# First units of four root-mean-square layers on rows before normalization, and rotary tables made in the short convolution

## The chip, the core and the metric

One core of a Trainium2 chip runs the whole program, once. The metric is the device time of one execution in microseconds (us). The engines are TensorE (PE in the rows; PEld is its weight load), VectorE (DVE), ScalarE (ACT), GpSimd (POOL) and SyncE (SP), which issues the transfers. Each has its own queue and works it off in order; they wait for each other on semaphores.

## The reference, cut to what matters

Two blocks follow each other on 256 tokens of width 1024. The first has four layers, each `x = x + mixer(rms_norm(x, g))`:

- a0 and a1, a conformer convolution: three projections to 2048 channels, `val * sigmoid(gate)`, a causal depthwise convolution of 31 taps, a layer norm over the channels, SiLU, a product with `silu(z)`, and an output projection;
- b, attention with 16 heads and forget gates: q and k are normalized per head, the cumulated log forget gates are added to the scores, and a gate z multiplies the heads' output;
- c, a short convolution: `y = b_gate * conv3(c_gate * u)`, times `silu(z)`, then the output projection.

`rms_norm(x, g)` is `x * rsqrt(mean(x*x) + 1e-6) * g`, with one factor for each token (row). So a projection of a normalized row is the projection of `x * g`, multiplied afterwards by the row's factor.

The second block has two layers of a token mixer (m0, m1), which uses rotary embeddings, and a gated convolution feed-forward (f0, f1). Their shifts, scales and gates come from `silu(c) @ w_ada`, 96 dot-product pieces that do not depend on x. All is computed in float32.

## The kernel before

**Weights.** All weights are cut into pieces of up to 128x1024 values, in an order that the planners (plan_a at line 202, plan_b at 225, plan_c at 254, plan_f at 341) write out. SyncE loads them into six raw buffers (load, 423). A piece of the kind "split" is used as two parts in a reduced format: ScalarE casts it to the high part (line 113, tile wh), VectorE subtracts that from the raw piece to get the low part (line 120, tile wl, in feed_dve, 476). A "plain" piece is used raw. An "ada" piece is a modulation product, one VectorE operation (ada, 490, tile raw<-raw,cb). The feeds look three pieces ahead by default, with five buffers of each part. TensorE multiplies high by high, high by low and low by high; so a unit of 128 outputs has 24 matmuls of 256 columns (unit, 516), or eight float32 matmuls for a plain unit (plain_unit, 566), each recorded twice. token_major (575) turns the roles round: twelve matmuls of 512 columns for each piece.

**Activations.** The layer's normalized, transposed input lies in XS as a high part xh(k) and a low part xl(k) for k from 0 to 7 (128 channels each). The residual stream X lies by tokens: half(tb, h) is token block tb, 512 channels of half h.

**A layer's entry.** The last output piece is added up in quarters (tb, h) in the order (0,0), (0,1), (1,0), (1,1) (out_last, 605). VectorE adds each to X (dve_residual, 760). ScalarE squares each quarter with its sum (act_squares), VectorE and ScalarE make the root R (act_root 632, dve_root 636), both scale X by it (act_rms 742, dve_rms 768), TensorE transposes the scaled rows (pe_entry, 685), and ScalarE and VectorE write xh and xl from PSUM, multiplied by g. For the a layers VectorE first writes a plain copy xn, from which the parts are made. Only then does the first unit start. While this goes on, TensorE runs filler matmuls on constants: 15 for b, 16 for c, 14 for a1. Before a0 it runs 24 on a constant tile.

**What follows.** In a, eight pairs of gate and value units feed VectorE and ScalarE, whose taps and GpSimd's make the convolution (dve_a 1056). In b (pe_b 1469), the forget-gate piece b.f comes first, then three value chunks v0 to v2, four k, four q. In c (pe_c 1780) each step i takes two channel groups through c, u, b and z units, with two output pieces, in banks that VectorE must have folded. In its last step, i = 14, one SiLU and one product serve both groups, and then come their high and low parts. The rotary tables are made in a0, after the low parts, by VectorE (dve_rope, 1242) and two Sin on ScalarE (act_rope, 1279), in tmp tiles. The order of the work of each engine is written out by hand in these functions.

A term that comes back below: b.v1.0 is the first piece of the second value chunk; "c.b0.1" the second unit of the b gate at i = 0.

Of the kernel before, what the change touches and what calls it, by code (L numbers as in the profile page):

```python
# [8 lines left out]
F32 = mybir.dt.float32  # L9
# [7 lines left out]
T = 256  # L17
D = 1024
# [183 lines left out]
def plan_a(j):  # L202
# [22 lines left out]
def plan_b():  # L225
    out = [("b.f", [("b_w_in", 0, 128 * k, 128, 4 * E, 16) for k in range(8) for _ in range(2)], "split")]
# [9 lines left out]
    for n in range(3):  # L236
        chunk("v", n, 2 * E, (1, 2, 3) if n else (3,))
    for which, base in (("k", E), ("q", 0)):
        for n in range(4):
            chunk(which, n, base, (1, 3))  # L240
# [13 lines left out]
def plan_c(u, u1):  # L254
# [6 lines left out]
    for i in range(0, 16, 2):  # L261
        if i == 0:
            for n in range(2):
                for kind, base in (("c", 2 * E), ("u", 0)):
                    out.append((f"c.{kind}0.{n}", tiles("c_w_in", 0, base + n * 128), "split"))
                    if kind == "u":
                        ada()
        for kind, base in (("c", 2 * E), ("u", 0), ("b", E), ("z", 3 * E)):
# [10 lines left out]
            ada()  # L279
# [97 lines left out]
class Net:  # L377
# [148 lines left out]
    def first_units(self, pe, X, normed, units):  # L526

        made = [(self.weights(pe, name), name, out) for name, out in units]
        for k in range(8):
            pe.wait_ge(*self.s["xlow"][X, k])  # L530
            for (i, wh, wl), name, out in made:
                h, l = wh[:, k * 128:(k + 1) * 128], wl[:, k * 128:(k + 1) * 128]
# [5 lines left out]
            for n in range(8):  # L538
                if X[0] in "mf" and self.turned_after(X, n) == k:
                    self.pe_turned_late(pe, X, normed, n)  # L540

# [62 lines left out]

    def out_last(self, pe, L, ks, Ys):

        for tb in range(2):
            for h in range(2):
                for k, Y in zip(ks, Ys):
                    ins = self.out_part(pe, L, k, ks[-1] + 1, Y, tb, h)  # L610
                    names = [(L, "sum", tb, h)] if k == ks[-1] else []
                    if tb and h:
                        names += [self.at[f"{L}.o{k}"], (L, "out", k)]
                    if names:
                        ins.then_inc(self.s["gemm"].up(*names), 1)
# [42 lines left out]
    def turned_at(self, L):  # L658

        if L == "a0":  # L660
            return [(4, 0), (5, 0), (6, 0), (0, 0), (1, 0), (2, 0), (3, 0), (5, 1)]
        if L == "b":
            return [(n, 0) for n in (6, 4, 5, 7, 0, 1, 2, 3)]
        if L == "a1":
            return [(n, 0) for n in (4, 5, 6, 7, 0, 1, 2, 3)]
        if L == "c":
            return [(n, 0) for n in (4, 6, 7, 0, 1, 2, 3)] + [(6, 1)]
        return [(6 if L[0] == "m" else 4, 0), (0, 0), (1, 0), (2, 0), (3, 0), (0, 1), (1, 1), (2, 1)]

    def turned_after(self, L, k):  # L670

        if L[0] in "mf":
            return k - 4 if k > 4 else None
        return 1 if k == 7 and L in ("a0", "c") else None
# [10 lines left out]
    def pe_entry(self, pe, L, normed):  # L685
# [3 lines left out]
        self.warm(pe, {"a0": 0, "a1": 14, "b": 15, "c": 16, "m0": 0, "m1": 18}.get(L, 11))  # L689
# [6 lines left out]
        if L[0] in "ac":  # L696
            for k in late:
                self.pe_turned_late(pe, L, normed, k)
# [20 lines left out]
    def read_turned(self, L, k):  # L719

        s = self.s
        if L[0] == "a":
            return s["norm"][L, "xn", k]
        if L[0] in "bc":
            return s["xlow"][L, k]
        return s["evac"][L, "h", k] if k % 2 else s["norm"][L, "h", k]

    def xnt(self, tb, h):
        return self.tmp[2 * tb + h]

    def act_squares(self, act, L, ready):
        s = self.s
        act.table(ACT.Sqrt)
        for tb in range(2):
            for h in range(1 if tb and L == "a0" else 2):
# [6 lines left out]
    def act_rms(self, act, L, ready, gname, plain):  # L742
        s, R = self.s, self.sums("R")
        self.act_squares(act, L, ready)
        act.wait_ge(*s["norm"][L, "root"])
        for n in range(2):
            act.activation(self.xnt(1, 0)[:, 256 * n:256 * n + 256], self.half(1, 0)[:, 256 * n:256 * n + 256], ACT.Identity,
                           scale=R[:, 1:2]).then_inc(s["shift"].up((L, n)), 1)
        act.activation(self.xnt(1, 1), self.half(1, 1), ACT.Identity, scale=R[:, 1:2]).then_inc(
            s["shift"].up((L, 2), (L, 3)), 1)  # L750
        for k in range(8):
            if plain:
                act.wait_ge(*s["norm"][L, "xn", k])
                act.copy(self.xh(k), self.xn()[:, k, :]).then_inc(s["high"].up((L, k)), 1)
            else:
                act.wait_ge(*s["turn"][L, "in", k])
                act.activation(self.xh(k), self.turned_tile(L, k), ACT.Identity, scale=self.c(gname, k)).then_inc(
                    s["high"].up((L, k)), 1)

    def dve_residual(self, dve, P):  # L760
        s = self.s
        for tb in range(2):
            for h in range(2):
                o = self.half(tb, h)
                dve.wait_ge(*s["gemm"][P, "sum", tb, h])
                dve.tt(o, o, self.ps[2 * tb + h], ALU.add).then_inc(s["resid"].up((P, tb, h)), 1)

    def dve_rms(self, dve, L, gname, plain):
        s = self.s
        q, a, v, R = self.sums("q").rearrange("p (b h) -> p b h", b=2), self.sums("a"), self.sums("v"), self.sums("R")  # L770
        dve.wait_ge(*s["square"][L, 1, 0])
        dve.ts(a, q[:, :, 0], 1.0 / D, 1e-6, ALU.mult, ALU.add).then_inc(s["norm"].up((L, "a")), 1)
        dve.wait_ge(*s["norm"][L, "a"])
        dve.wait_ge(*(s["norm"][L, "q"] if L == "a0" else s["square"][L, 1, 1]))
        dve.stt(v, q[:, :, 1], 1.0 / D, a, ALU.mult, ALU.add).then_inc(s["norm"].up((L, "v")), 1)
        self.dve_root(dve, R, v, self.sums("d"), L)
        dve.wait_ge(*s["norm"][L, "root"])
        for h in range(2):
            dve.ts(self.xnt(0, h), self.half(0, h), R[:, 0:1], None, ALU.mult, None).then_inc(
                s["norm"].up((L, "x", 0, h)), 1)  # L780
        for k in range(8):
            dve.wait_ge(*s["turn"][L, "in", k])
            if plain:
                dve.ts(self.xn()[:, k, :], self.turned_tile(L, k), self.c(gname, k), None, ALU.mult, None).then_inc(
                    s["norm"].up((L, "xn", k)), 1)
            else:
                dve.wait_ge(*s["high"][L, k])
                dve.stt(self.xl(k), self.turned_tile(L, k), self.c(gname, k), self.xh(k).bitcast(F32), ALU.mult,
                        ALU.subtract).then_inc(s["xlow"].up((L, k)), 1)
        for k in range(8) if plain else ():  # L790
            dve.wait_ge(*s["high"][L, k])
            dve.tt(self.xl(k), self.xn()[:, k, :], self.xh(k).bitcast(F32), ALU.subtract).then_inc(
                s["xlow"].up((L, k)), 1)
# [50 lines left out]
    def pe_a(self, pe, j):  # L844
        s, A = self.s, f"a{j}"
        XN = self.xn()
        if j == 0:
            w = self.tmp[5][:, 0:128]
            pe.wait_ge(*s["fill"][0])
            for _ in range(24):  # L850
# [2144 lines left out]
```

## Time and profile before

| | us |
|---|---|
| median of 3 runs | 1757.71 (1756.76 to 1759.4) |
| the profiled execution, own time | 1757.96 |
| its span, first to last instruction | 1756.1 |
| TensorE busy | 1723.6 |
| VectorE busy | 1477.3 |
| ScalarE busy | 1094.9 |
| GpSimd busy | 289.7 |

Busy time counts filler matmuls too. A row's "idle before" is time in which the engine had nothing to run, with the operation whose end released it. In rows of a timeline the first two numbers are the start, from the start of the span, and the time to the end of the last of the instructions that the row joins. Since a matmul's modelled end overlaps the next one's start, the distance of two starts is what one costs.

### The profile page before, as it was taken

The numbers are of one execution on the slowest core, as the hardware profiler recorded it, in microseconds if no ns is written. First come the engines' busy times: TensorE is split into PE (matmuls) and PEld (weight loads), VectorE is DVE, ScalarE is ACT, GpSimd is POOL, SyncE is SP. The second block draws the span as 40 slices with busy tenths as digits, with TensorE's granted clock in tenths as the row PEclk, the third lists the DMA queues.
The fourth block names the chain that finished last, engine by engine and source line by source line (L and its number), as shares of the span: only waits on it lengthen the run. The fifth ranks groups of instructions, "written<-read, shape, count | busy, mean of one in ns | idle before, by whom it ended". The sixth has DMA issues, their size and how long they took to land.

```text
span 1756.1 us, 28780 instructions
## 1 busy us (share of the span) xinstructions
PE 1723.6 (98%) x10458; PEld 1510.2 (86%) x10458; DVE 1477.3 (84%) x2861; ACT 1094.9 (62%) x2149; POOL 289.7 (16%) x396
## 2 busy tenths in 40 slices
PE   9999999999999999999999999999999999999997
PEld 8888888888888888788898988988888998988886
DVE  7998878877789999788987698789987688789887
ACT  6888665555455555578875555566566656566664
POOL 3996000000000000078920000002000200002000
PEclk9999999999999999999999999999999999999999
DMA  6455568855558888544465654546764544546662
GB/s 239 153 157 172 170 220 305 266 179 183 201 196 315 289 304 310 170 154 136 153 194 157 224 185 133 170 148 189 253 223 146 168 156 127 174 143 188 222 187 78
DMA packets 92734, 339.49 MB, mean 193 GB/s; under 512 B 10288, under 2 KB 10672, under 8 KB 91952
## 3 DMA queue, kind: packets, MB, share of 16 engines
q1 hardware_dynamic: 92592, 337.64, 59.0%
q8 instruction: 84, 1.38, 0.3%
q14 instruction: 58, 0.48, 0.1%
HBM read 336.55 MB, written 1.05 MB: 192 GB/s over the span
## 4 chain that ended last, share of the span: by engine, by line
PE 74%; DVE 12%; ACT 8%; issue 4%; POOL 2%; DMA 0%; ACTq 0%; DVEq 0%; POOLq 0%
PE ps L104 72%; DVE wl L120 4%; ACT tmp L110 4%; ACT wh L113 2%; PE ps L107 2%; POOL B L120 2%; DVE tmp L130 1%; DVE raw L130 1%; DVE tmp L120 1%; DVE B L120 1%; DVE sm L142 1%; ACT os L113 1%; ACT B L110 1%; DVE os L120 1%; DVE X L130 0%
## 5 line engine op out<-in xcount | busy, mean ns | idle before, releaser
L104 PE MATMUL ps<-XS,wh 128*128 128x256 f32 (+2 forms) x3184 | 779.2, 327 | 8.6 <-DVE wl L120 4.7
L120 DVE TENSOR_TENSOR wl<-raw,wh 128x1024 fp32r<-128x1024 f32 x471 | 576.2, 1237 | 99.7 <-ACT wh L113 97.5
L104 PE MATMUL ps<-XS,wl 128*128 128x256 f32 x2152 | 581.7, 281 | 0.0
L104 PEld LDWEIGHTS ps<-XS,wh 128*128 128x128 f32 (+1 forms) x3184 | 525.3, 190 | 65.1 <-issue 19.0
L113 ACT CAST wh<-raw 128x1024 fp32r<-128x1024 f32 x471 | 479.5, 1044 | 102.3 <-PE ps L104 93.0
L104 PEld LDWEIGHTS ps<-XS,wl 128*128 128x128 f32 x2152 | 408.4, 190 | 11.5
L120 POOL TENSOR_TENSOR B<-B,tmp 128x236 f32<-128x236 f32 (+11 forms) x368 | 247.4, 716 | 642.0 <-ACT tmp L110 627.1
L104 PE MATMUL ps<-wh,os 128*128 128x512 f32 x864 | 280.8, 393 | 5.4 <-DVE os L120 4.1
L130 DVE SCALAR_TENSOR_TENSOR ps<-B,C,ps 128x253 f32<-128x253 f32 (+17 forms) x560 | 216.3, 465 | 2.8 <-ACT ps L110 2.8
L104 PE MATMUL ps<-B,raw 128*128 128x256 f32 x992 | 218.6, 380 | 0.0
L104 PEld LDWEIGHTS ps<-B,raw 128*128 128x128 f32 x992 | 186.7, 190 | 27.5 <-issue 2.9
L104 PEld LDWEIGHTS ps<-wh,os 128*128 128x128 f32 x864 | 162.9, 189 | 39.1 <-DVE os L120 5.0
L110 ACT ACTIVATE B<-ps 128x256 f32<-128x256 f32 (+2 forms) x216 | 95.4, 452 | 157.5 <-PE ps L104 157.2
L104 PE MATMUL ps<-wh,XS 128*128 128x512 f32 x576 | 179.4, 391 | 0.0
L110 ACT ACTIVATE tmp<-B,C 128x236 f32<-128x236 f32 (+11 forms) x368 | 153.8, 478 | 34.8 <-POOL B L120 34.0
L104 PE MATMUL ps<-wl,os 128*128 128x512 f32 x432 | 168.8, 391 | 0.0
L120 POOL TENSOR_TENSOR X<-X,B 128x512 f32<-128x512 f32 x24 | 42.1, 1754 | 700.5 <-PE ps L104 700.5
L104 PEld LDWEIGHTS ps<-wh,XS 128*128 128x128 f32 x576 | 107.2, 188 | 21.6
L130 DVE SCALAR_TENSOR_TENSOR raw<-raw,cb 128x1024 f32<-128x1024 f32 x96 | 116.3, 1217 | 0.0
L104 PE MATMUL ps<-wl,XS 128*128 128x512 f32 x288 | 112.3, 390 | 0.0
L104 PEld LDWEIGHTS ps<-wl,os 128*128 128x128 f32 x432 | 81.6, 189 | 16.7
L130 DVE SCALAR_TENSOR_TENSOR tmp<-ps,C,tmp 128x254 f32<-128x254 f32 (+1 forms) x176 | 76.1, 476 | 10.9 <-ACT tmp L110 8.8
(168 smaller groups left out, 1659.0 us busy)
## 6 DMA issues: line engine op xcount, KB each, us to landing
raw<-in_w SPq DMA_DIRECT2D x628, 512.0 KB, 4.5
B<-in_ln SPq DMA_DIRECT2D x4, 1024.0 KB, 6.7
C<-in_cst SPq DMA_DIRECT2D x1, 1103.5 KB, 9.1
X<-in_x SPq DMA_DIRECT2D x2, 512.0 KB, 4.5
out_x<-X SPq DMA_DIRECT2D x4, 256.0 KB, 2.5
cb<-in_cb SPq DMA_DIRECT2D x1, 512.0 KB, 13.7
pos<-in_pos SPq DMA_DIRECT2D x1, 160.0 KB, 5.3
raw<-in_w SPq DMA_DIRECT2D x1, 128.0 KB, 2.0
```

What stands on the lines that cost most here:

```text
L104: return NOTHING if self.e is None else self.e.matmul(*a, **k)
L107: return NOTHING if self.e is None else self.e.transpose(*a)
L110: return NOTHING if self.e is None else self.e.activation(*a, **k)
L113: return NOTHING if self.e is None else self.e.copy(*a)
L120: return NOTHING if self.e is None else self.e.tensor_tensor(o, a, b, op)
L130: return self.e.scalar_tensor_tensor(out=o, in0=a, scalar=s, in1=b, op0=op0, op1=op1, **k)
L142: return NOTHING if self.e is None else self.e.tensor_reduce(o, a, AX, ALU.max)
```

## The change

- Order of the quarters for the layers ahead of b, c and a1: (0,0), (1,0), (0,1), (1,1), with four raw transposes (k = 0 to 3) of the un-normalized X ahead of the last quarter. The other four come inside the first units. The filler of b, c and a1 goes; a0 has 18 instead of 24.
- The first units multiply `x * g` without the row factor: g0 in the a layers, v0 in b, the first units of c and u in c. Their results are multiplied by the factor afterwards: in b per token where v0 leaves PSUM, in a by an extra product ahead of the sigmoid, in c by the factor's square after `c * u`.
- The factor is spread over the partitions by two matmuls (pe_row_root) and copied by ScalarE. VectorE multiplies a kept copy of `x * g` by it (dve_normed), and in b and c xh and xl are then overwritten with the parts of the normalized rows while the first units read them (signals "bn", "cn").
- b.f moves from ahead of v0 to behind v1, and the forget row's work with it. In a1 v0's two pieces become plain.
- In c the ada pieces of i = 0 and two each of i = 4 and i = 8 are taken out of the order; they come later.
- The rotary tables move from a0 to c (VectorE at i = 4 and 8, ScalarE at i = 6), in tile G.
- At i = 14 in c the two groups are taken separately through SiLU, product, high and low parts.

```diff
 def plan_a(j):
-        first = "split" if j else "plain"
-        two("g", p, E, *[first if p == 1 else "plain"] * 2)
-        two("v", p, 0, "split" if p else first, "plain" if p else first)
+        two("g", p, E, *["split" if j and p == 1 else "plain"] * 2)
+        two("v", p, 0, "split" if p else "plain", "plain")
...
 def plan_c(u, u1):
-                    if kind == "u":
-                        ada()
...
-            ada()
+            if i and (i not in (4, 8) or kind in "uz"):
+                ada()
...
+    def quarters(self, L):
+        return ((0, 0), (1, 0), (0, 1), (1, 1)) if L in ("a0", "b", "c") else ((0, 0), (0, 1), (1, 0), (1, 1))
+
     def out_last(self, pe, L, ks, Ys):
+        for tb, h in self.quarters(L):
+            if tb and h and L in ("a0", "b", "c"):
+                for k in range(4):
+                    self.pe_raw_turned(pe, {"a0": "b", "b": "c", "c": "a1"}[L], k)
...
+    def pe_raw_turned(self, pe, L, k):
+        s, h, a = self.s, k // 4, (k % 4) * 128
+        if L != "a0" and k >= 4:
+            pe.wait_ge(*s["resid"][self.prior(L), 1, 1])
+        for tb in range(2):
+            pe.wait_ge(*(s[f"x{tb}"][0] if L == "a0" else s["resid"][self.prior(L), tb, h]))
+            ins = pe.transpose(self.turned_tile(L, k)[:, tb * 128:tb * 128 + 128], self.half(tb, h)[:, a:a + 128],
+                               self.c("ident", 0, 128))
+        ins.then_inc(s["turn"].up((L, "in", k)), 1)
+
+    def pe_row_root(self, pe, L):
+        pe.wait_ge(*self.s["shift"][L, "raw", 3])
+        pe.wait_ge(*self.s["norm"][L, "root"])
+        self.spread(pe, 7, self.sums("R"), (L, "R"))
+
+    def act_normed_high(self, act, L, k):
+        act.wait_ge(*self.s["norm"][L, "xn", k])
+        act.wait_ge(*(self.s["gemm"]["b.v0", k // 2] if L == "b" else self.s["gemm"]["c", "read", k]))
+        act.copy(self.xh(k), self.taken(k)).then_inc(self.s["high"].up((L + "n", k)), 1)
...
 def pe_b(self, pe):
-        self.pe_entry(pe, "b", self.xnt)
-        self.unit(pe, self.ps[6][0:32, 0:T], "b.f", "b", 32)
...
+        for kp in range(4):
+            self.token_major(pe, self.b_chunk(0), "b.v0", "b", (kp,))
+            if kp == 0:
+                for k in range(4, 8):
+                    self.pe_raw_turned(pe, "b", k)
+            if kp == 1:
+                self.pe_row_root(pe, "b")
+        pe.wait_ge(*s["evac"]["b", "R"])
+        self.token_major(pe, self.b_chunk(1), "b.v1", "bn")
+        self.unit(pe, self.ps[0][0:32, 0:T], "b.f", "bn", 32)
+        self.token_major(pe, self.b_chunk(2), "b.v2", "bn")
...
 def dve_b(self, dve):
+        self.dve_residual(dve, "a0", 0, 0)
+        self.dve_residual(dve, "a0", 1, 0)
+        self.dve_residual(dve, "a0", 0, 1)
+        self.dve_turned_low(dve, "b", 0)
+        self.dve_turned_low(dve, "b", 1)
+        self.dve_residual(dve, "a0", 1, 1)
+        self.dve_first_squares(dve, "b")
+        self.dve_all_squares(dve, "b")
+        self.dve_turned_low(dve, "b", 2)
+        self.dve_row_root(dve, "b")
+        for k in range(3, 8):
+            self.dve_turned_low(dve, "b", k)
+        self.dve_joined(dve, "b", 0)
+        self.dve_joined(dve, "b", 1)
...
+        self.feed_dve(dve, "b.v0.0")
+        dve.wait_ge(*s["evac"]["b", "R"])
+        for k in range(8):
+            self.dve_normed(dve, "b", k)
+        self.dve_normed_low(dve, "b", 0)
+        self.dve_normed_low(dve, "b", 1)
+        self.feed_dve(dve, "b.v0.2")
...
 def act_c(self, act):
+            if i == 14:
+                for n in range(2):
+                    wide("z", i, n)
+                    act.wait_ge(*s["folded"][f"c.z{i}.{n}"])
+                    act.activation(zs[:, n * T:n * T + T], self.c_wide("z", n), ACT.Silu).then_inc(
+                        s["evac"].up(("c", "z", i, n)), 1)
+                    self.feed_act(act, f"c.o{13 + n}")
+                    split(i, (14 + n,))
+                self.feed_act(act, "c.o15")
+                break
...
 def dve_c(self, dve):
+            if i == 4:
+                self.dve_rope(dve)
+            if i == 8:
+                self.dve_rope_spread(dve)
...
+                dve.tt(cs, self.ps[5], cs, ALU.mult).then_inc(s["evacd"].up(("c", "cu")), 1)
...
+                dve.tt(pairs, pairs, square.unsqueeze(1).to_broadcast([128, 2, T]), ALU.mult).then_inc(
+                    s["evacd"].up(("c", "u", i)), 1)
```

## Rows read from the trace of the kernel before

**Rows 1.** The page, part 1: busy time of each engine and share of the span.

```profile
PE 1723.6 (98%) x10458; PEld 1510.2 (86%) x10458; DVE 1477.3 (84%) x2861; ACT 1094.9 (62%) x2149; POOL 289.7 (16%) x396
```

**Rows 2.** Timeline, 220 to 236 us, entry of b: start, us, engine, line, operation, idle before.

```profile
222.54 2.73 DVE L120 TENSOR_TENSOR X<-X,ps 128x512 f32<-128x512 f32 x4 [1.04 <-PE ps L104]
...
224.39 3.51 PE L104 MATMUL ps<-C 128*128 128x128 f32 x30
...
225.31 0.63 ACT L110 ACTIVATE tmp<-X 128x512 f32<-128x512 f32 x1
...
227.89 1.97 PE L107 MATMUL ps<-C,tmp 128*128 128x128 f32 x16
228.78 3.00 ACT L110 ACTIVATE XS<-ps,C 128x256 fp32r<-128x256 f32 x8
...
229.97 0.39 PE L104 MATMUL ps<-XS,wh 128*32 128x256 f32 x2
```

**Rows 3.** Windows (busy of PE, PEld, DVE, ACT, POOL), then VectorE's timeline, layer b.

```profile
241.00:252.00 11.00, 11.00 (x51) 8.92 (x50) 9.70 (x14) 4.12 (x5) 0.00 (x0) 1.00 0.71 220
...
266.62 0.69 DVE L133 COPY B<-ps 128x512 f32<-128x512 f32 x1 [0.36 <-PE ps L104]
```

**Rows 4.** The page, part 5 (count, busy, mean ns, idle before), and VectorE's timeline in a0.

```profile
L120 DVE TENSOR_TENSOR wl<-raw,wh 128x1024 fp32r<-128x1024 f32 x471 | 576.2, 1237 | 99.7 <-ACT wh L113 97.5
...
L130 DVE SCALAR_TENSOR_TENSOR raw<-raw,cb 128x1024 f32<-128x1024 f32 x96 | 116.3, 1217 | 0.0
...
13.23 2.76 DVE L120 TENSOR_TENSOR XS<-B,XS 128x256 fp32r<-128x256 f32 x8
```

**Rows 5.** Timelines of VectorE and TensorE, 494 to 530 us, entry of c.

```profile
495.92 2.48 DVE L120 TENSOR_TENSOR X<-X,ps 128x512 f32<-128x512 f32 x4
...
503.69 0.47 PE L104 MATMUL ps<-XS,wh 128*128 128x256 f32 x2
...
504.48 0.40 PE L104 MATMUL ps<-XS,wh 128*128 128x256 f32 x2
...
517.77 0.68 DVE L120 TENSOR_TENSOR tmp<-ps,tmp 128x512 f32<-128x512 f32 x1
```

**Rows 6.** Timeline and a window, 719 to 746 us: tail of c, entry of a1.

```profile
719.63 0.42 DVE L120 TENSOR_TENSOR B<-ps,B 128x256 f32<-128x256 f32 x1
...
726.35 0.50 PE L104 MATMUL ps<-wh,os 128*128 128x512 f32 x1 [4.05 <-DVE os L120]
...
727.20:730.60 3.40, 3.40 (x10) 2.63 (x9) 0.00 (x0) 0.00 (x0) 0.00 (x0) 0.50 0.00 1
...
738.84 7.07 PE L104 MATMUL ps<-B,raw 128*128 128x256 f32 x32
```

**Rows 7.** Timelines of three engines in a0: its start, and the end of its convolution.

```profile
11.29 20.88 PE L104 MATMUL ps<-B,raw 128*128 128x256 f32 x96
...
20.18 1.06 ACT L110 ACTIVATE cb<-cb 128x1024 f32<-128x1024 f32 x1 [5.12 <-DMA cb<-in_cb]
21.26 0.72 ACT L110 ACTIVATE rope<-tmp 32x256 f32<-32x256 f32 x2
...
26.20 0.68 DVE L120 TENSOR_TENSOR B<-ps,tmp 128x512 f32<-128x512 f32 x1
...
162.93 0.41 PE L104 MATMUL ps<-B,C 128*32 128x256 f32 x2 [2.01 <-ACT tmp L110]
```

**Rows 8.** Timelines of VectorE and TensorE in f0: the gated product of successive iterations.

```profile
1238.97 0.69 DVE L120 TENSOR_TENSOR tmp<-tmp 128x512 f32<-128x512 f32 x1
...
1242.75 0.47 PE L104 MATMUL ps<-wh,os 128*128 128x512 f32 x1 [0.45 <-DVE wl L120]
...
1256.29 0.69 DVE L120 TENSOR_TENSOR tmp<-tmp 128x512 f32<-128x512 f32 x1
...
1305.73 0.68 DVE L120 TENSOR_TENSOR tmp<-tmp 128x512 f32<-128x512 f32 x1
...
1322.35 0.68 DVE L120 TENSOR_TENSOR tmp<-tmp 128x512 f32<-128x512 f32 x1
```

More of the change, by code:

```diff
@@ L225, in plan_b @@
 def plan_b():
-    out = [("b.f", [("b_w_in", 0, 128 * k, 128, 4 * E, 16) for k in range(8) for _ in range(2)], "split")]
+    out = []
     u = iter(range(48))
@@ L237, in plan_b @@
         chunk("v", n, 2 * E, (1, 2, 3) if n else (3,))
+        if n == 1:
+            out.append(("b.f", [("b_w_in", 0, 128 * k, 128, 4 * E, 16) for k in range(8) for _ in range(2)], "split"))
     for which, base in (("k", E), ("q", 0)):
@@ L734, in act_squares @@
         for tb in range(2):
-            for h in range(1 if tb and L == "a0" else 2):
+            for h in range(2):
                 act.wait_ge(*ready(tb, h))
@@ L740, in act_squares @@
         self.act_root(act, self.sums("d"), self.sums("v"), L)
[L742 to L793, printed above, removed]
@@ L869, in pair, with taken, first_gates @@
                     self.unit(pe, o, f"{A}.{kind}{p}.{n}", A)
+        def taken(n, k):
+            pe.wait_ge(*s["norm" if k in (1, 2) else "shift"][A, "raw", k])
+            i = self.at[f"{A}.g0.{n}"]
+            return pe.matmul(self.ps[4][:, n * T:n * T + T], self.raw(i)[:, k * 128:(k + 1) * 128], self.taken(k),
+                             start=k == 0, stop=k == 7)
+        def first_gates():
+            for n in range(2):
+                pe.wait_ge(*self.landed(self.at[f"{A}.g0.{n}"]))
+                for k in range(8):
+                    ins = taken(n, k)
+                    if j and n == 0 and k == 3:
+                        for late in range(4, 8):
+                            self.pe_raw_turned(pe, A, late)
+                ins.then_inc(s["gemm"].up(self.at[f"{A}.g0.{n}"], f"{A}.g0.{n}"), 1)
+                if n == 0:
+                    self.pe_row_root(pe, A)
         def stats(q):
@@ L1618, in act_b @@
                     self.act_root(act, self.b_norm(i)[2], self.b_norm(i)[1], ("b", i))
+                if j == 2 and kp == 1:
+                    forget()
             if j < 3:
@@ L1781, in pe_c @@
         s = self.s
-        self.pe_entry(pe, "c", self.xnt)
         for n in range(2):
@@ L1807, in pe_c, with last_unit @@
         self.pe_out_last(pe, "c", [15])
+    def last_unit(self, pe, out, name):
+        i, wh, wl = self.weights(pe, name)
+        for k in range(8):
+            h, l = wh[:, k * 128:(k + 1) * 128], wl[:, k * 128:(k + 1) * 128]
+            pe.matmul(out, h, self.xh(k), start=k == 0, stop=False)
+            pe.matmul(out, h, self.xl(k), start=False, stop=False)
+            pe.matmul(out, l, self.xh(k), start=False, stop=k == 7).then_inc(
+                self.s["gemm"].up(*([i, name, ("c", "read", k)] if k == 7 else [("c", "read", k)])), 1)
     def c_bank(self, kind):
@@ L1932, in dve_c @@
                 self.feed_dve(dve, f"c.z{i}.{n}")
+            if i == 14:
+                for n in range(2):
+                    half = slice(n * T, n * T + T)
+                    wide("z", i, n)
+                    self.feed_dve(dve, f"c.o{13 + n}")
+                    dve.wait_ge(*s["evac"]["c", "z", i, n])
+                    dve.wait_ge(*s["evacd"]["c", "b", i])
+                    dve.tt(ac[:, half], ac[:, half], zs[:, half], ALU.mult).then_inc(s["conv"].up(("c", "y", 14 + n)), 1)
+                    self.dve_low(dve, "c", 14 + n, ac[:, half])
+                self.feed_dve(dve, "c.o15")
+                break
             wide("z", i, 0)
```

421 lines of the change are left out of this document (298 added, 123 removed).

## The prediction

> **What bounds the kernel now.** I read first the page's busy times: TensorE is busy 98% of the span, VectorE 84%, so TensorE's queue is the bound almost everywhere and VectorE stands close behind it [rows 1]. Then I read the timeline of each layer entry, because a filled engine can be filled with nothing. At the entry of layer b, 30 filler matmul records (15 filler matmuls, two records each) start at 224.39, 16 transposes follow at 227.89 and the first matmul that computes something starts at 229.97 [rows 2]. The reader is to see the chain behind this: residuals from 222.54, squares (the last at 225.31), root, scaling, transposes, and high parts from 228.78. Entries c and a1 look the same: real work starts at 503.69 [rows 5] and 738.84 [rows 6], the first of them after residuals that start at 495.92. Last come the places where TensorE waits openly: 4.05 us at 726.35 for the last output pieces of c, followed by a stretch at granted clock 0.50 [rows 6]; 2.01 us at 162.93, where a0's convolution, carried by VectorE, ends late [rows 7]; and 0.45 us at 1242.75 in f0 [rows 8]. A VectorE queue with little idle time decides what an earlier TensorE is worth: in the window 241 to 252 it is busy 9.70 of 11.00 us [rows 3].
>
> **Prices.** A high part on ScalarE takes 3.00/8 = 0.375 us, a residual 2.73/4 = 0.68 us, a square with its accumulator 0.67 us (0.63 plus issue) [rows 2]. VectorE's 128x256 two-tensor operation takes 2.76/8 = 0.345 us; the low part of a weight piece 1.24 us, about 1.14 when back to back; a modulation piece ("ada") 1.22, about 1.14 back to back [rows 4]. Sixteen transposes take 1.97 us [rows 2], so four k (eight transposes) take about 0.92. A piece of twelve 512-column matmuls takes four times the 0.68 us at which the residuals follow its quarters, 2.73 [rows 2]. A plain unit takes 7.07/2 less the overlap of its last record, 3.36 us [rows 6]; two steps of three 256-column matmuls take 0.79 us, the first late by 0.07, so 0.36 a step and 2.9 a split unit of eight [rows 5].
>
> **Part 1, start of a0.** Raw transposes can start when x has landed, near 7.4 us, so g0.0 could start near 8.5 instead of 11.29, some 2.8 us earlier on TensorE, less 0.46 for a spread [rows 7]. But the convolution starts with v0's gating product at 26.20. Its gate follows the Silu of the broadcast input, which waits for its transfer until 20.18, then two Sin of 0.72 us together, at 21.26 [rows 7]. The transfer stays; the two Sin leave. So the convolution starts 0.7 us earlier, and since VectorE carries that convolution and TensorE waits for its end [rows 7], the end moves by 0.7 us. The rotary operations that leave VectorE lay under this transfer wait and are worth nothing here. Value: **-0.7**; bounds 0 and -2.3, the whole of TensorE's gain.
>
> **Part 2, entry of b.** Quarters of the last output now come in the order (0,0), (1,0), (0,1), then four raw transposes, then (1,1), ending at 225.55 instead of 224.6. High and low of k = 0 and 1 are done at 224.65 and 225.5, so b.v0.0 starts at 225.55, 4.4 us earlier than 229.97. Inside v0 stand 0.92 us of transposes and 0.46 us for spreading the root (four records, about a quarter of the sixteen). Root chain: squares end at 227.1, root at 228.9, behind it five low parts, two joins (0.69) and the low of v0.3, which ends at 234.6; then eight normalizations (2.76) to 237.3, two new lows to 238.0, one ada to 239.15, and the low of v1.0 to 240.3. TensorE ends v0 at 237.9 and waits 2.4 us for v1.0. The same queue delays v1.2 (two lows, another weight low, two lows, v0's evacuation, two lows, an ada, then its own low: 246.4 against 245.8): 0.65 us. Then b.f (2.9) and v2 end at 265.7; before, v2 ended just ahead of the copy at 266.62 [rows 3], say 266.3. Added on VectorE are 18 operations of 0.345 = 6.2 us, less two scalings; removed waiting on TensorE is paid back as waiting for weights. Value: **-0.6**. Bounds: -3.7 (VectorE keeps up, no wait) and +1.1 (see rival A). The forget row moves from v0 into v2: its 2.6 us of VectorE and 3.9 us of ScalarE latency end at 263, and k0.0's low at 265.5, just ahead of TensorE.
>
> **Part 3, entry of c.** Residuals start at 495.92 as before, because a weight low stands ahead of them [rows 5]. ScalarE has one cast more in its look-ahead (c.c0.1 in place of an ada), which puts its first square at 497.1. Then the first pair of units starts at 498.9 and is interleaved with four k of transposes: eight steps of 0.72 plus 0.92, end 505.65. Before, it ended at 503.69 + 5.76 = 509.45. Spread 0.46, two units of 2.9: 511.9. From here VectorE is behind again: normalization 507.2 to 510, one weight low, eight new lows to 513.9, the square of the root to 514.2, so c.b0.1's low is ready at 515.35 (wait 0.7), and c times u needs a second product, 0.65 us, ready at 518.9 (wait 0.8). c.z0.0 starts at 519.0 against 515.28 + 5.6 = 520.9. Value **-1.9**; bounds -3.4 and -0.9. The c times u product stands at 517.77 before [rows 5], so in spite of an earlier TensorE it ends later: that is the row to look at. The two adas of this stretch are gone, which is what lets VectorE recover.
>
> **Part 4, rotary tables in c.** 4.6 us on VectorE at i = 4, against two adas (2.3 us) taken out there; the burst stands under three pieces of look-ahead. I take **+0.2**, between 0 and +2.3 (no cover). At i = 8, 1.3 us against 2.3: nothing.
>
> **Part 5, tail of c and entry of a1.** Now z14's two halves go separately. The fold of z14.0 at 719.63 stays, because two adas stand ahead of it [rows 6]. The half Silu follows at 720.1, then the cast of o14 (to 721.5), its low (722.7), the product (723.1), high (723.5), low (723.95): o14 starts at 724.0 instead of 726.35. The second half: fold 724.35, Silu 724.75, cast and low of o15 to 727.0, product, high, low to 728.2, so after o14 (726.7) TensorE waits 1.5 us. The last output ends at 731.0 plus 0.92 of transposes plus a 0.15 wait for the residual, 732.15, and g0.0 starts there: 6.7 us before 738.84. Of these 6.7, transposes 4 to 7 return 0.92, the spread 0.46, and v0's two units turned plain 2 x 0.42 = 0.85. v0.1 ends at 747.0 instead of 751.5; VectorE's gating product is at 747.3. Value **-4.4**, of which 1.7 is the stretch at half clock (3.4 us at 0.50 [rows 6]) that a wait split in two (1.9 and 1.5 us) should not bring. Bounds -5.5 and -2.5.
>
> **Part 6, eight adas more in f0.** The plan takes eight out of c, and m0 already has all it can hold; f0 then has two at every i from 8 to 20. In f0 VectorE's gated product repeats every 17.32 us with two adas (1238.97 to 1256.29) and every 16.62 us without (1305.73 to 1322.35), and TensorE shows the wait at 1242.75 [rows 8]. Four iterations change: 4 x 0.70 = **+2.8**. Bounds +1.5 and 8 x 1.22 = +9.8.
>
> **Sum.** -0.7 - 0.6 - 1.9 + 0.2 - 4.4 + 2.8 = -4.6 us. The profiled execution took 1757.96 us (span 1756.1), 0.25 above the median; so 1753.4 us.
>
> After the open wait of 4.05 us TensorE ran 3.4 us at a granted clock of 0.50, that is 1.2 of 2.4 GHz [rows 6].
> The Trainium skill ("TensorE: Matmul & The Clock Gate", part 1) says that "the default state is throttled, and activity releases the throttle", which speaks against dropping the filler. By that rule each of the three entries could cost a half-clock stretch, and the sum would be about +0.5 rather than -4.6; no row shows one of these entries without filler.
>
> **Rivals.**
> A. The clock falls once the filler is gone, most likely after the new wait of 2.4 us in b: half of 3.4 us, +1.7, so 1755.1; at all three entries +5.1, 1758.5. For: after 4.05 us of waiting it fell [rows 6]. Against: this wait is shorter, and real work is dense on both sides. Chance 0.20.
> B. VectorE keeps up at the entries of b and c (orders of work that hide more than I count): -3.1 and -1.5 more, 1748.8. For: 1.3 us of 11 idle in v1 [rows 3]. Against: added operations stand ahead of the weight lows. Chance 0.15.
> C. Slower: in f0, at 1237 to 1355, the adas stand ahead of the output's low parts and are paid whole, +9.8 instead of +2.8: 1760.4. It decides once VectorE has no idle left within an iteration. For: the wait at 1242.75. Against: the period grew by 0.70 only. Chance 0.08.
> D. The entries don't do what they say: first units wait for lows queued behind the root chain, so each starts no earlier, while spreads (1.85), plain units (0.85) and f0 (2.8) are paid, the tail keeping -2.8: +2.7, 1760.7. Against: lows 0 and 1 stand ahead of the root in the queue. Chance 0.07.
>
> **Numbers.** The forecast, 1753.4, has 0.50. Its own bounds give about 2 us either way. A measurement tells 0.2% (3.5 us) from no change, so faster means under 1754.2. That holds most of the forecast (0.34), all of B (0.15) and a little of A: 0.52. Slower means over 1761.2: the ends of C and D, 0.07. The rest is 0.41. The range reaches to B (1749.0) and past A (1757.5); C and D and a tail of B are left out.
>
> **What would show it.** No filler and first units near 225.6, 498.9 and 732.2 less what a0 and earlier entries gained; a TensorE wait for a weight low at b.v1.0 of about 2.4 us, two of 0.7 to 0.8 in c's first iteration; at c's end two waits of 1.9 and 1.5 us and no clock of 0.50; four more waits of 0.6 us in f0. It is wrong if first units start late, if b shows no wait, or if the f0 period stays at 16.62.

## The result, and the profile after

The changed kernel took **1762.17 us** (median of 9 runs, 1759.63 to 1764.21) beside 1757.42 of the kernel before (9 runs, 1756.33 to 1759.4): a ratio of **1.0026**, 95% interval 1.0017 to 1.0035. The forecast was 1753.4. Every ratio in this document is to runs of the kernel before taken beside the kernel in question; their median moves between 1756.65 and 1757.9, so of two kernels the ratios are to be compared, not the medians. The profiled execution took 1762.74 us (span 1761.0, 4.9 more than before).

The page, part 1, as in [rows 1]:

```profile
PE 1719.5 (98%) x10356; PEld 1502.1 (85%) x10356; DVE 1488.3 (85%) x2896; ACT 1100.1 (62%) x2180; POOL 286.4 (16%) x396
```

TensorE does 4.1 us less work than before in a span that is 4.9 us longer: it waits 9 us more. I first laid the landmarks of the two traces beside each other. The length of a stretch, from one layer's first residual to the next one's, in us:

```
stretch                before    after    difference
start to a0 residual   222.54   220.00      -2.5
to b residual          273.38   281.82      +8.4
to c residual          235.77   232.16      -3.6
to a1 residual         218.09   216.54      -1.5
to m0 residual         201.68   202.59      +0.9
to f0 residual         194.43   198.43      +4.0
to m1 residual         202.54   201.57      -1.0
```

What is left, the last layer, is 0.2 longer. b is 9 us off the forecast, the other stretches 2 us at most. TensorE's timeline of after at the entry of b, to be read against [rows 2], and then its idle times in b:

```profile
221.16 1.24 PE L107 MATMUL ps<-C,X 128*128 128x128 f32 x8
...
222.94 0.69 PE L104 MATMUL ps<-wh,XS 128*128 128x512 f32 x2
...
238.01 0.70 PE L104 MATMUL ps<-wh,XS 128*128 128x512 f32 x2 [2.56 <-DVE wl L120]
...
264.66 0.70 PE L104 MATMUL ps<-wh,XS 128*128 128x512 f32 x2 [2.96 <-DVE wl L120]
270.09 1.19 PE L104 MATMUL ps<-wh,XS 128*128 128x512 f32 x2 [2.42 <-DVE wl L120]
```

The entry does what it says: v0.0 starts 2.9 us after the first residual (220.00), where before the first matmul that computes something took 7.4. The wait of 2.56 for v1.0's low is the 2.4 of the forecast. The two waits at 264.66 and 270.09 stand nowhere in it. (The expectations below count a wait from one start to the next, less a matmul's own time; by that count these three are 2.72, 3.12 and 2.58 us.) The releaser, VectorE's low, is only the last link. VectorE's timeline of after, then ScalarE's:

```profile
255.38 1.22 DVE L120 TENSOR_TENSOR wl<-raw,wh 128x1024 fp32r<-128x1024 f32 x1
256.52 0.47 DVE L125 TENSOR_SCALAR tmp<-ps,C 32x256 f32<-32x256 f32 x1
...
263.28 1.23 DVE L120 TENSOR_TENSOR wl<-raw,wh 128x1024 fp32r<-128x1024 f32 x1 [5.16 <-ACT wh L113]
...
266.18 0.41 DVE L130 SCALAR_TENSOR_TENSOR tmp<-tmp 32x256 f32<-32x256 f32 x1
...
268.74 2.34 DVE L120 TENSOR_TENSOR wl<-raw,wh 128x1024 fp32r<-128x1024 f32 x2
```

```profile
252.97 1.04 ACT L113 CAST wh<-raw 128x1024 fp32r<-128x1024 f32 x1
257.02 0.42 ACT L110 ACTIVATE tmp<-tmp 32x256 f32<-32x256 f32 x1 [3.00 <-DVE tmp L125]
257.45 1.28 ACT L110 ACT_TABLE_LOAD   x1
258.75 0.42 ACT L110 ACTIVATE tmp<-tmp 32x256 f32<-32x256 f32 x1
259.18 1.28 ACT L110 ACT_TABLE_LOAD   x1
...
260.91 1.28 ACT L117 ACT_TABLE_LOAD   x1
262.21 2.94 ACT L113 CAST wh<-raw 128x1024 fp32r<-128x1024 f32 x3
```

Read them as a chain. VectorE makes y, the forget row's input, at 256.52, behind two lows and an ada of its feed. ScalarE has waited 3.00 us for it and now runs Abs, Exp and Ln with three table loads, 5.2 us. Only then does it cast the weights (262.21). VectorE stood idle for 5.16 us for want of those casts. Its row work from 266.18 on then stands ahead of the next lows. In the kernel before, the same chain ran on ScalarE from 234.39 to 239.58, behind two casts and a wait of only 0.31 us for y, and TensorE waited for nothing from 215 to 300 us:

```profile
231.63 2.04 ACT L113 CAST wh<-raw 128x1024 fp32r<-128x1024 f32 x2
...
234.39 0.42 ACT L110 ACTIVATE tmp<-tmp 32x256 f32<-32x256 f32 x1 [0.31 <-DVE tmp L125]
...
239.58 2.00 ACT L113 CAST wh<-raw 128x1024 fp32r<-128x1024 f32 x2
```

The clock adds to this. Windows of after over its stretches at half the clock (columns as in [rows 3]; the last three are granted clock, share of the transfers, GB/s):

```profile
238.90:242.30 3.40, 3.40 (x10) 2.64 (x9) 3.40 (x7) 0.00 (x1) 0.00 (x0) 0.50 0.74 266
269.70:273.10 3.40, 3.01 (x7) 2.47 (x8) 3.37 (x7) 0.48 (x1) 0.00 (x0) 0.51 0.57 172
1006.90:1010.30 3.40, 3.40 (x19) 3.40 (x18) 2.11 (x5) 0.64 (x2) 0.00 (x0) 0.50 0.96 352
```

The first two stand at waits of b: one begins 0.9 us behind the wait of 2.56 us, the other inside the wait of 2.42 us. Each costs up to 1.7 us. The third explains m0's +0.9: over the profiles with the same m0, its stretch takes 202.6 to 202.9 us with such a stretch in it and 201.5 to 201.7 without. The kernel before had two in the same span, at 164 and at 727.2 [rows 6], so the net is one more.

### The profile page after: what moved, and what is told of

The parts are those of the page before. It is cut to its first block, busy times and chain, and to the rows that moved or that the text cites. A ratio compares the mean times of both kernels' runs of the same rounds, so it can differ in the third digit from the quotient of the medians.

```text
span 1761.0 us, 28640 instructions
## 1 busy us (share of the span) xinstructions
PE 1719.5 (98%) x10356; PEld 1502.1 (85%) x10356; DVE 1488.3 (85%) x2896; ACT 1100.1 (62%) x2180; POOL 286.4 (16%) x396
## 4 chain that ended last, share of the span: by engine, by line
PE 66%; DVE 16%; ACT 9%; issue 5%; POOL 2%; DMA 1%; SPq 0%; ACTq 0%; DVEq 0%; POOLq 0%
PE ps L104 65%; DVE wl L120 6%; ACT tmp L110 3%; ACT wh L113 3%; POOL B L120 2%; DVE raw L130 2%; PE ps L107 2%; DVE tmp L130 2%; DVE tmp L120 1%; DVE B L120 1%; ACT B L110 1%; ACT os L113 1%; DMA cb<-in_cb 1%; DVE X L130 1%; DVE sm L142 1%
## 5 line engine op out<-in xcount | busy, mean ns | idle before, releaser
L104 PEld LDWEIGHTS ps<-XS,wh 128*128 128x128 f32 (+1 forms) x3152 | 521.2, 190 | 65.4 <-issue 19.5
L104 PE MATMUL ps<-B,raw 128*128 128x256 f32 x1024 | 226.1, 380 | 0.0
L104 PEld LDWEIGHTS ps<-B,raw 128*128 128x128 f32 x1024 | 192.9, 190 | 28.1 <-issue 2.9
```

Of the source, the lines that this page charges most:

```text
L104: return NOTHING if self.e is None else self.e.matmul(*a, **k)
```

## The experiments

**Whose lateness is it?** Theory 1: the order on ScalarE. Theory 2: VectorE's whole work, or the transfers.

```diff
 # e1_y_first, VectorE, layer b
+                if j == 2 and kp == 0:
+                    forget()
                 if j < 11 or kp < 2:
                     self.feed_dve(dve, f"{name}.{kp}")
 ...
-                if j == 2 and kp == 0:
-                    forget()
```

> VectorE makes y (the forget gate's pre-activation) ahead of the feed of v2.0 instead of behind it; nothing else moves. Theory 1 (order on ScalarE: the forget row's Abs, Exp and Ln with three table loads stand ahead of the casts of v2.3 and k0.0): y comes at about 254 instead of 256.5 us, ScalarE's 3.0 us wait for it goes, TensorE's wait of 3.12 us ahead of v2.3 falls to about 0.5, the 2.58 us ahead of k0.0 stays; some 2.7 us less, about 1759.5. Theory 2 (VectorE's whole work up to v2.3, or the transfers into the raw buffers, is what is late, whatever ScalarE's order): both waits stay within 0.5 us, the time stays at 1762.

Measured: 1758.98 us (ratio to before 1.0004, 0.9995 to 1.0014). TensorE's idle time in b, from the waits between 215 and 300 us, falls from the first line (after) to the second (this run):

```profile
PE ps L104 <- DVE wl L120: 7.9, 3, 3.0
```

```profile
PE ps L104 <- DVE wl L120: 5.0, 2, 2.6
```

One instruction of 0.47 us, put two lows and an ada earlier, gives some 3 us. The wait of 2.45 us ahead of k0.0 stays, as expected. Theory 2 falls as the account of the whole loss; b_order_only below shows what VectorE's load adds.

```diff
 # e2_no_tables, ScalarE, the forget row
-            act.activation(e1, e1, ACT.Exp, scale=-1.0)...
+            act.activation(e1, e1, ACT.Identity, scale=-1.0)...
-            act.activation(e1, e1, ACT.Ln, bias=1.0)...
-            act.table(ACT.Sqrt)
+            act.activation(e1, e1, ACT.Identity, scale=-1.0)...
```

> Exp and Ln of the forget row are replaced by Identity and the table load behind them is left out, so the forget term is not computed; it takes three table loads of 1.28 us off ScalarE. Theory 1: the casts of v2.3 and k0.0 come 3.8 us earlier, the wait of 3.12 us goes and the one of 2.58 shrinks to 1.5 to 2, with one half-clock stretch (1.7 us) less if it falls under 2: 4 to 6 us less, 1756 to 1758. Theory 2: no change, since ScalarE is not what VectorE waits for: 1762.

Measured: 1755.81 us (0.9993, 0.9984 to 1.0002), a little below the 1756 to 1758 expected; this kernel leaves the forget term out. The wait ahead of v2.3 is gone, the one ahead of k0.0 is 1.70 us. ScalarE's timeline: the chain is one row of 1.32 us and the casts come right behind.

```profile
254.75 1.32 ACT L110 ACTIVATE tmp<-tmp 32x256 f32<-32x256 f32 x3 [2.55 <-DVE tmp L125]
255.97 1.98 ACT L113 CAST wh<-raw 128x1024 fp32r<-128x1024 f32 x2
```

**Can order alone mend it?**

```diff
 # late_forget, ScalarE and VectorE
-            act.table(ACT.Sqrt)          (at the end of the forget row's chain)
-                if j == 2 and kp == 1:
+                if j == 2 and kp == 2:
+                    self.feed_act(act, f"{name}.2", 4)
                     forget()
+                if j == 3 and kp == 1:
+                    act.table(ACT.Sqrt)
 # VectorE: forget() ahead of feed v2.0 as above; the feed of v2.3 looks 2 ahead
-                if j == 2 and kp == 2:
-                    forgotten()
+            if j == 2:
+                forgotten()
```

> The forget row's three ScalarE instructions are put behind the casts of v2.3 and k0.0, the table load for Sqrt behind the feed of k0.1, VectorE's y ahead of the feed of v2.0 and its scan behind the feed of v2.3 and k0.0. The work is the same, its order alone differs. Theory 1: both waits (3.12 and 2.58 us) fall below 0.7 and the half-clock stretch at 269.7 goes: 6 to 7 us less, 1755 to 1756. Theory 2: the waits stay, 1762.

Measured: 1755.96 us (0.9993, 0.9984 to 1.0002), about 6 us less than the changed kernel with the same work. The wait ahead of v2.3 is gone, and so is every stretch at half clock in b. A wait of 1.75 us stayed, now ahead of k0.1, whose cast (264.69) still stood behind the chain, so the expectation "below 0.7" was met by one wait and missed by the other.

```diff
 # b_as_before
-    pe_b, act_b, dve_b, plan_b of the changed kernel
+    pe_b, act_b, dve_b, plan_b, entry and order of quarters of the kernel before
```

> Layer b's entry, its order and the place of its forget row as in the kernel before; everything else of the change stays. Theory 1 (the change's loss lies in b alone, 5.9 us from a0's first residual to b's against 2.6 gained ahead of it): b takes as long as before, and what the other parts gained shows: 8.4 us less than the changed kernel at b's end, so 1753.5 to 1755, faster than before. Theory 3 (what is gained ahead of b is given back later whatever b does, by f0's eight adas and the half clocks in the middle): 1757 or more.

Measured: 1754.65 us (0.9986, 0.9977 to 0.9995). With b as before, the other parts show their gain, some 2.5 us: the loss lies in b, and theory 3 falls.

```diff
 # b_repaired, beside VectorE's y first, as above
 # ScalarE
-                if j == 2 and kp == 1:
+                if j == 2 and kp == 3:
                     forget()
-            act.table(ACT.Sqrt)          (at the end of the chain)
+                if j == 3 and kp == 3:
+                    act.table(ACT.Sqrt)
 # VectorE
+                if j == 3 and kp == 1:
+                    forgotten()
-        for k in range(8):
+        for k in range(4):
             self.dve_normed(dve, "b", k)
 ...
         self.feed_dve(dve, "b.v0.2")
+        for k in range(4, 8):
+            self.dve_normed(dve, "b", k)
 # plan_b
-        chunk("v", n, 2 * E, (1, 2, 3) if n else (3,))
+        chunk("v", n, 2 * E, ((), (2, 3), (1, 2, 3))[n])
-            if h > 1 and h % 2 or h in (4, 6, 10, 12, 14):
+            if h > 1:
```

> The late order of the forget row taken further, with b's new entry kept: ScalarE's chain behind the cast of k0.1 instead of k0.0, its table load for Sqrt behind the feed of k0.3, VectorE's scan behind the feed of k0.1; rows 4 to 7 are normalized behind the feed that holds v1.0's low (four times 0.38 us of VectorE off its way); the adas of v0 and of v1.1 go to z2 and z8 (1.14 us of VectorE each). Theory 1 (what starves TensorE in b is the order of VectorE's and ScalarE's instructions, no lack of engine time): the waits of 2.72, 0.41 and 1.91 us that the late order still had go to under 0.7 in all, with no half clock there: 4 to 5 us less than the late order's 1756.0, so 1751 to 1752.5, faster than both kernels. Theory 4 (VectorE is full from 235 to 262 us, and what is moved comes back as a wait at k0.0 to k1): no more than 1 us less, 1755 to 1756.

Measured: **1752.4 us** (0.9978, 0.9969 to 0.9987), faster than the kernel before. In the timeline of ScalarE two more casts now stand ahead of the chain and its cost is covered:

```profile
257.12 1.05 ACT L113 CAST wh<-raw 128x1024 fp32r<-128x1024 f32 x1 [1.60 <-DMA raw<-in_w]
...
259.90 1.05 ACT L113 CAST wh<-raw 128x1024 fp32r<-128x1024 f32 x1 [1.73 <-PE ps L104]
260.85 0.41 ACT L110 ACTIVATE tmp<-tmp 32x256 f32<-32x256 f32 x1
261.28 1.28 ACT L110 ACT_TABLE_LOAD   x1
```

All that is left of TensorE's idle time in b, in the waits between 215 and 300 us:

```profile
PE ps L104 <- DVE wl L120: 0.3, 1, 0.3
```

```diff
 # b_order_only, against b_repaired
-        chunk("v", n, 2 * E, ((), (2, 3), (1, 2, 3))[n])
+        chunk("v", n, 2 * E, (1, 2, 3) if n else (3,))
-            if h > 1:
+            if h > 1 and h % 2 or h in (4, 6, 10, 12, 14):
```

> The repaired kernel with the adas of v0 and v1.1 back where the change has them: order alone is repaired. If b's waits come from order alone, b_repaired's gain stays: the waits in b are at most 1 us more, 1752.5 to 1753.5. If VectorE is also full from 235 to 262 us (it stood idle there for 2.4 us only in the late order), the two adas of 1.14 us come back as waits of 1 to 2.3 us at v1.0 and behind it: 1753.5 to 1755.

Measured: 1754.89 us (0.9984, 0.9976 to 0.9993), the second case, though its interval overlaps that of b_repaired; the waits are 1.2 us ahead of v1.0 and 1.3 ahead of v1.2. From a0's residual to b's, one profile each, the late order takes 275.4 us, this one 273.4, the repaired 272.3: order gave 2.0 of its last step, the two adas 1.1. The kernel before took 273.4 as well. So with its order mended the new entry of b only breaks even; what b gains, 1.1 us, comes with the two adas moved, and whether the old entry would gain as much by moving them was not tried. VectorE is close to full there, as the forecast had it: 24.3 of 27.0 us between 235 and 262.

**The clock behind a wait** (rival A of the forecast).

```diff
 # v1_filler, TensorE, layer b
         pe.wait_ge(*s["evac"]["b", "R"])
+        self.warm(pe, 11, 2)
         self.token_major(pe, self.b_chunk(1), "b.v1", "bn")
```

> The changed kernel with 11 matmuls of 128 columns ahead of b's v1, which write where nothing is read, in the stretch in which TensorE waits 2.7 us for v1.0's low. The rival of the forecast by which the clock falls behind this new wait: the half clock at 238.9 us goes, 1.7 us less, about 1760.5, with the other waits as they were. If the half clock comes from something else than this wait, it stays, 1762.

Measured: 1759.36 us (1.0014, 1.0006 to 1.0023); by the ratios (1.0014 against 1.0026) that is a gain of some 2 us, and the intervals overlap, so it is likely, not certain. The profile has no stretch at half clock at 239, but one at 263.5, behind the wait for v2.3 that stays. The same wait of 2.6 us at v1.0 stands in five profiles without filler; the clock fell behind it in two (the changed kernel and adas_in_c) and not in three (e1_y_first, e2_no_tables, late_forget). So one profile without the stretch does not show that the filler kept it away.

**The tail of c.**

```diff
 # tail_alone: the kernel before, in act_c and dve_c
+            if i == 14:
+                for n in range(2):
+                    ... one channel at a time: wide, half Silu, feed of o14 + n, product, high, low
+                break
```

> The kernel before with one part of the change: the last pair of channels in c is finished one channel at a time. If the forecast's part 5 is right, the wait of 4.2 us ahead of o14 becomes two (1.9 and 1.5), no half clock follows, and the time falls by 1.1 and 1.7: 1754.5 to 1755.5. Rival (the clock falls behind two waits as behind one): 1756.5.

Measured: 1756.97 us beside 1756.65 (1.0000, 0.9991 to 1.0008): no gain that shows, against 1.1 of waits and 1.7 of clock expected (1754.5 to 1755.5). The interval leaves room for a gain of 1.6 us, not for both. TensorE's timeline shows that the wait did split as forecast, against 4.05 us in [rows 6]:

```profile
723.26 0.50 PE L104 MATMUL ps<-wh,os 128*128 128x512 f32 x1 [1.65 <-DVE os L120]
727.48 0.50 PE L104 MATMUL ps<-wh,os 128*128 128x512 f32 x1 [1.16 <-DVE os L120]
```

c is 2.0 us shorter, and m0, which nothing touched, 1.3 us longer, with a stretch at half clock at 1002.9 that the profile of before lacks. Part 5's 1.7 for the clock was read from one profile, and a stretch at half clock that is absent in one place can turn up in another; that the edit itself moved it is not shown.

**The eight adas.**

```diff
 # adas_in_c
-            if i and (i not in (4, 8) or kind in "uz"):
-                ada()
+            ada()
 # and one behind each c.u0.n
 # c_half_back: b_repaired with
+            if i:
+                ada()
```

> The changed kernel with the eight adas that it moved from c to f0 back in c; b stays as changed. If they cost in f0 what the trace shows (six waits of 0.61 us in place of two, and 4.0 us more from m0's residual to f0's, of which 1.0 is gained back to m1's) and c hides them as before: f0 falls by 4, the end by 3, about 1759. Rival (c's VectorE is full since the rotary tables are made there): c's part grows by 2 to 3 us, 1762 again.

> The repaired kernel with four of the eight adas back in c, those of the second and fourth pair of channels after the first; c's entry stays free of adas. f0 then holds four fewer: its time falls by 4 of 0.5 to 0.6 us. If what made c grow by 6 us with all eight back is the entry (waits of 0.98, 0.94 and 2.84 us there), c stays and the end is 1.5 to 2 us earlier, 1750.5 to 1751. If c has no room further on either (waits of 1.37 and 1.0 us at 576 and 585 us of that run), c grows by 2 and the time stays at 1752.4.

Measured: adas_in_c 1764.1 us (1.0042, 1.0029 to 1.0056). f0 falls by 4.0 and m1 gives 1.0 back, as expected, but c takes 238.7 us in place of 232.2, 6.5 more, of which up to 1.7 is a stretch at half clock at 523.65. TensorE's timeline of that run:

```profile
514.37 0.47 PE L104 MATMUL ps<-XS,wh 128*128 128x256 f32 x2 [0.82 <-DVE wl L120]
...
524.05 0.76 PE L104 MATMUL ps<-XS,wh 128*128 128x512 f32 x1 [2.68 <-DVE wl L120]
```

The expectation that c hides them failed, and the rival was too low as well. c_half_back: 1754.05 us (0.9976, 0.9967 to 0.9985), the same as the repaired kernel. Its profile has f0 2.7 shorter, m1 0.9 longer and c 1.7 longer: these four adas cost in c what they cost in f0. Taking the four at c's entry out was right (by difference they make the rest of the 6.5); for the four at i = 4 and 8 it made no difference.

```diff
 # adas_in_a1: b_repaired, plan_a(1)
+        if 2 <= k < 10:
+            out.append(ada_piece(1, next(u)))
 # adas_in_m0: b_repaired, plan_m(0), behind each bs piece and o0 to o3
+            ada()
```

> The repaired kernel (b_repaired) with the eight adas that went from c to f0 put into a1, one behind each of the pieces o2 to o9. VectorE is free for 6 to 9 us there (23.6 us busy of 30, 22.3 of 25), while in f0 each ada costs TensorE a wait of 0.61 us. If what an ada costs is set by how full VectorE is where it stands: f0 falls by 4.0 and m1 gains 1.0 less, a1 stays, 3 us less than the repaired kernel's 1752.4: 1749 to 1750. Rival (it is the raw buffers and their transfers, not VectorE's time, that f0's waits come from, and a1's last stretch has transfers at 0.58 to 0.68 of the engines): a1 grows by 2 to 3 us, 1752.

> The same with the eight adas at m0's end (behind the pieces bs0 to bs6 and o0 to o3), where VectorE is busy 30.9 us of 42 and the transfers 0.55. VectorE's room decides: 3 us less than 1752.4 again, 1749 to 1750. Rival (raw buffers and transfers): m0 grows by as much, 1752.

Measured: 1769.99 us (1.0074, 1.0062 to 1.0086) and 1758.66 (1.0010, 1.0002 to 1.0019). Both lose, and by more than their rivals allowed: a1 grew by 19.5 us in the one, m0 by 7.8 in the other, each with some 3.1 us back in f0 and m1 together. TensorE in a1 waits once every second output piece, four times in a row by the same length, each time with a stretch at half clock behind:

```profile
915.47 0.47 PE L104 MATMUL ps<-wh,os 128*128 128x512 f32 x1 [2.79 <-DVE wl L120]
925.58 0.47 PE L104 MATMUL ps<-wh,os 128*128 128x512 f32 x1 [2.79 <-DVE wl L120]
```

The window says whether an engine is full: VectorE 29.08 of 40.00 us, transfers 0.65 of the time, the clock 0.83.

```profile
912.00:952.00 40.00, 28.84 (x95) 21.90 (x95) 29.08 (x43) 16.66 (x26) 0.00 (x0) 0.83 0.65 217
```

Neither is. The transfers come in bursts and then stop (mean busy tenths over 912 to 950 us):

```profile
DMA  8670569999840008899897000369999940006699
```

An ada takes one of six raw buffers in turn and holds it until VectorE comes to it in order, and the next pieces' transfers wait for that. That this ring makes the cycle of 10.11 us fits the gaps in the transfers; it was not tried by itself, with a seventh buffer for instance, and stays open. "VectorE has room there" is refuted as a reason for placing one.

## Why the prediction was wrong

**The step that failed** is in part 2: "The forget row moves from v0 into v2: its 2.6 us of VectorE and 3.9 us of ScalarE latency end at 263, and k0.0's low at 265.5, just ahead of TensorE." It priced the moved chain as a latency and did not ask what is queued behind it on ScalarE, nor when its input y comes. The chain occupies that queue for 5.2 us with the load for Sqrt, after 3.0 us of waiting, ahead of the casts of v2.3 and what follows; v2.3's low, not k0.0's, was the first to be late. Price: waits of 2.96 and 2.42 us that the forecast had at nothing, and a stretch at half clock at the second of them; together up to 7.1 of the 9.0 us by which b misses. The stretch at half clock at 238.9, rival A's, is up to 1.7 more. e1_y_first, e2_no_tables and late_forget each take part of it away by a different handle.

**Part 1** held. a0's convolution started 2.0 us earlier (24.18 for 26.20), but 1.1 of that is the transfer of the broadcast input: its Silu starts at 19.07, where [rows 7] have 20.18, and in the other profiles of the same a0 between 19.02 and 20.51. From the Silu to the first gating product it takes 5.11 us in place of 6.02: 0.9 for the forecast's 0.7.

```profile
19.07 1.06 ACT L110 ACTIVATE cb<-cb 128x1024 f32<-128x1024 f32 x1 [0.33 <-DMA cb<-in_cb]
...
24.18 0.68 DVE L120 TENSOR_TENSOR B<-ps,tmp 128x512 f32<-128x512 f32 x1
```

**Part 2, the rest**, held roughly: b loses 8.4 in the trace; without 5.4 of unforeseen waits and up to 3.4 of clock that is -0.4, against -0.6. The foreseen wait ahead of v1.2 (0.65) is absent here, where v1 began at half clock; in the profiles whose clock stayed up it came, 0.21 us in e1_y_first and 1.29 in b_order_only.

**Part 3** held. The units start at 504.68, 2.9 us after the first residual, and the two waits that the forecast named came, ahead of b0.1 and z0.0:

```profile
521.01 0.47 PE L104 MATMUL ps<-XS,wh 128*128 128x512 f32 x1 [0.28 <-DVE wl L120]
524.64 0.47 PE L104 MATMUL ps<-XS,wh 128*128 128x512 f32 x1 [0.61 <-issue]
```

c.z0.0 starts 22.8 us after the residual; the forecast had 23.1 (519.0 less 495.92), and 25.0 for the kernel before. The first output piece of c confirms it: 47.47 us after the residual before (543.39), 45.24 after (547.06), so 2.2 gained for the 1.9 forecast.

```profile
543.39 0.39 PE L104 MATMUL ps<-wh,os 128*128 128x512 f32 x1
```

```profile
547.06 0.39 PE L104 MATMUL ps<-wh,os 128*128 128x512 f32 x1
...
550.17 0.47 PE L104 MATMUL ps<-XS,wh 128*128 128x512 f32 x1 [0.22 <-DVE wl L120]
```

**Part 4** took +0.2, and the tables cost about 1.0, within its bounds. The short wait at 550.17 takes 0.4 of the lead of 2.2. Then the rotary work holds VectorE from 564.67 to 569.03, and TensorE waits for a fold behind it. At the output piece behind that (83.69 us after the residual before, 82.87 after) 0.8 is left:

```profile
564.67 0.27 DVE L139 MEMSET rope<- 64x256 f32 x1
...
568.74 0.29 DVE L125 TENSOR_SCALAR G<-G 32x256 f32<-32x256 f32 x1
```

```profile
570.68 0.50 PE L104 MATMUL ps<-XS,wh 128*128 128x512 f32 x1 [0.77 <-DVE tmp L120]
...
584.69 0.39 PE L104 MATMUL ps<-wh,os 128*128 128x512 f32 x1
```

That the adas taken out at i = 4 and 8 left room for the tables is borne out by c_half_back, where their return costs 1.7 us.

**Part 5** came near in its waits (1.64 and 1.16 for 1.9 and 1.5) and in its sum in the trace: 2.5 in c's last stretch, from the output piece of channel 13 on, and 1.5 in a1, against 4.4.

```profile
728.76 0.50 PE L104 MATMUL ps<-wh,os 128*128 128x512 f32 x1 [1.64 <-DVE os L120]
732.97 0.50 PE L104 MATMUL ps<-wh,os 128*128 128x512 f32 x1 [1.16 <-DVE os L120]
```

But tail_alone shows that the 1.7 for the clock should not have been booked whole: over many runs that edit gives nothing that shows.

**Part 6** has the right mechanism, and its sum, +3.0 against +2.8, is near by luck: f0 loses 4.0, and m1 gives back 1.0 that was not forecast. Four periods grow, as forecast, three of them by 0.7; the fourth took 15.49 us before, not 16.62, and grows by 1.85. f0's products now repeat every 17.33 to 17.35 us in all five periods from 1240.62 to 1327.30. Before, then after:

```profile
1273.61 0.68 DVE L120 TENSOR_TENSOR tmp<-tmp 128x512 f32<-128x512 f32 x1
...
1289.10 0.69 DVE L120 TENSOR_TENSOR tmp<-tmp 128x512 f32<-128x512 f32 x1
```

```profile
1309.97 0.69 DVE L120 TENSOR_TENSOR tmp<-tmp 128x512 f32<-128x512 f32 x1
1327.30 0.69 DVE L120 TENSOR_TENSOR tmp<-tmp 128x512 f32<-128x512 f32 x1
```

**The rivals.** A was half right: the clock fell at b's waits, but filler can be missed only at the first of them, up to 1.7 us of the loss (the other belongs to the forget row's chain); at the entries of c and a1 it did not fall. B, C and D did not happen. None of them was what happened, a serial chain of another engine ahead of the casts. The Trainium skill ("TensorE: Matmul & The Clock Gate", part 1) says that "activity releases the throttle"; read as the forecast read it, each entry without filler was at risk. The trace agrees for b alone, where TensorE had waited 2.56 us, and not for c and a1, where the clock stayed up.

## What to carry to other kernels

When a chain moves past a point in the program, price it on every queue that it is issued to: the wait for its input and its whole length, table loads too, stand ahead of whatever that engine does next for somebody else. The repair is order: start its input early, put the casts of the next pieces ahead of it, and its reader last (1762.2 to 1756.0 with not one operation less; 1754.9 with the order taken further, and 1752.4 with two adas moved as well). An idle share of an engine does not say that a piece of work fits there: eight adas cost 3 us in f0 and 19.5 us in a1.

## What the runs showed that was not expected

- A wait of this length does not decide the clock by itself. TensorE's wait at the end of a0's convolution is 2.0 us in twelve of the fourteen profiles; the granted clock fell to 0.50 behind it in six of these. Behind v1.0's 2.6 us it fell in two of five. Runs of the changed kernel spread over 4.6 us. A stretch of 3.4 us at half clock is worth up to 1.7 us, a third of this change, and can't be credited to an edit from one profile.
- A table load is 1.28 us and the next ACTIVATE starts 0.02 us behind it (257.45 to 258.75): dear for its place in the queue, not for any drain around it.
- The same ada of 1.22 us on VectorE lengthens the kernel by 0.4 us in f0 (3.0 for eight), as much in c behind its entry (1.7 for four), 1.0 at m0's end (7.8 for eight) and 2.4 in a1's output (19.5 for eight, of which four stretches at half clock make up to 6.8).
